# Five of eight gate pairs of two branches as seven block products for eight

## The chip, the cores and the metric
## The reference
Two layers over 512 prompt rows and 64 sample rows (together T = 576 columns), 1024 wide. A layer computes a projection `h @ w_in` into three branches (mLSTM, gMLP, sliding-window attention) and three sets of 1024 gates; each branch is projected to 1024, gated and summed; then an output projection and a SwiGLU feed-forward network (FFN) follow. What the change touches are the gates:

```python
gates = jax.nn.sigmoid(gl).reshape(B, S, N_BRANCH, D_MODEL)
merged = (gates[:, :, 0] * (y_ml @ p['w_br_mlstm'])
          + gates[:, :, 1] * (y_sg @ p['w_br_gmlp'])
          + gates[:, :, 2] * (y_sw @ p['w_br_swa']))
x = x + g1 * rms_norm(merged @ p['w_out'], p['g_post_mix'])
```

`gl` is the part of `h @ w_in` from column 3848 on: three times 1024 columns.

## The kernel before
Features lie on the 128 partitions, the 576 rows of both inputs along them in two halves of 288. A float32 product is made of three products of rounded parts: high by high, high by low, low by high. So each weight chunk (1024 x 128, 512 KB) is loaded by SyncE's queue into one of two raw buffers, split by GpSimd into a high part (L882) and a low part (L885), and used by TensorE in 8 x 3 x 2 = 48 matmuls of 128x288 (`main`, through `feature_group`, L971). A chunk's raw buffer is loaded again when its split is done. A gate chunk `g1_3` is the fourth 128 features of the second branch's gates. Gates come in pairs. Behind a pair stands its branch chunk: 512 x 256 weights, split in the same way, used in two groups of 24 matmuls (`br1_2` and `br1_3`).

For each gate, ScalarE takes a tanh of PSUM into the buffer `tmp` (L1899; a sigmoid is made from it), and VectorE merges: (tanh + 1) x branch in PSUM (L2886), and that added to `mid` (L2313, the line of a helper which records every tensor_tensor). In the second branch (sliding window, in the code `sw`, number 1) a spatial product of the third branch (`spatial`, L1625, `z0` to `z3`) follows each pair of gates; ScalarE writes its bias to PSUM first (`z_bias`, L2077), VectorE multiplies the result, ScalarE and VectorE round it into `y_hi` and `y_lo`.

PSUM has four units of two banks each, used in a fixed ring (`MIX` gives the order, `UNIT` the unit). Every engine has its own program, in order; semaphores join them. The order of each is written out in the code.

In the FFN stage most of the first projection runs in another form: for a pair of 128-feature outputs and two halves of the columns, the 2x2 block product of weights (blocks a11, a12, a21, a22; 512 KB each pair half) by activations is made of seven block products p1 to p7 (Winograd's form of Strassen's) in place of eight. Its operands are sums and differences of weight blocks (s1 to s4, made for each pair by VectorE) and of activation quarters (t1 to t4, made once a layer), each split into a high part (ScalarE, L2138 and L2151 for weights, L2125 for activations) and a low part (GpSimd for a11, a12, a22, L898; VectorE for the sums). A product is 4 x 3 matmuls of 288 columns (`product`, L1063), a pair 84; partial results are copied from PSUM by ScalarE (L2165) and added by VectorE.

## Time and profile before
| what | value |
|---|---|
| median of three runs | 2061.83 us (2061.35 to 2062.76) |
| profiled execution | 2064.86 us |
| its span, first to last instruction | 2063.1 us |
| TensorE busy | 2030.5 us (98%), 16241 matmuls |
| VectorE, ScalarE, GpSimd busy | 987.8, 624.9, 1064.4 us |
| mean granted TensorE clock | 0.998 |
| plain matmuls (L971) on the chain that ended last | 43% of the span |

The profile lists groups of instructions by line, with their busy time and the idle time before them; the chain that ended last, which is what the time is made of; and, on query, instructions in order of time. Matmuls overlap, so one of 128x288 is listed with 0.29 us though one follows the other every 0.133 us. Times are from the start of the span.

### The profile page before, as it was taken

The numbers are of one execution on the slowest core, as the hardware profiler recorded it, in microseconds if no ns is written. First come the engines' busy times: TensorE is split into PE (matmuls) and PEld (weight loads), VectorE is DVE, ScalarE is ACT, GpSimd is POOL, SyncE is SP. The second block draws the span as 40 slices with busy tenths as digits, with TensorE's granted clock in tenths as the row PEclk, the third lists the DMA queues.
The fourth block names the chain that finished last, engine by engine and source line by source line (L and its number), as shares of the span: only waits on it lengthen the run. The fifth ranks groups of instructions, "written<-read, shape, count | busy, mean of one in ns | idle before, by whom it ended". The sixth has DMA issues, their size and how long they took to land.

```text
span 2063.1 us, 38507 instructions
## 1 busy us (share of the span) xinstructions
PE 2030.5 (98%) x16241; PEld 1959.7 (95%) x16241; DVE 987.8 (48%) x1645; ACT 624.9 (30%) x1358; POOL 1064.4 (52%) x562
## 2 busy tenths in 40 slices
PE   8999999999999999999999999999999999999998
PEld 6998898999999999999999989889999999999997
DVE  5223466422257535647563235663223573647473
ACT  4111224110134333425532121340102343525253
POOL 0443454567763745363734534546687546354543
PEclk9999999999999999999999999999999999999999
DMA  9746232233351333233535342222233413232332
GB/s 358 259 137 52 63 82 59 68 83 86 90 182 42 126 121 92 83 92 93 174 121 174 62 63 76 62 59 75 82 103 89 148 43 91 82 89 85 94 93 77
DMA packets 299771, 211.93 MB, mean 103 GB/s; under 512 B 13728, under 2 KB 293840, under 8 KB 296400
## 3 DMA queue, kind: packets, MB, share of 16 engines
q1 hardware_dynamic: 292848, 205.94, 34.8%
q10 hardware_dynamic: 6752, 3.53, 0.7%
q8 instruction: 129, 2.11, 0.4%
q14 instruction: 42, 0.34, 0.1%
HBM read 204.65 MB, written 4.07 MB: 101 GB/s over the span
## 4 chain that ended last, share of the span: by engine, by line
PE 93%; DMA 2%; DVE 2%; POOL 1%; ACT 1%; issue 1%; SPq 0%; DVEq 0%; POOLq 0%; ACTq 0%
PE ps L971 43%; PE ps L1063 19%; PE ps L999 13%; PE ps L1083 3%; DMA raw<-in_w_in 2%; PE ps L1089 2%; PE ps L1216 2%; PE ps L1131 1%; PE ps L1595 1%; PE ps L1558 1%; PE ps L1573 1%; PE ps L1431 1%; PE ps L1259 1%; PE ps L1110 1%; PE ps L1446 1%
## 5 line engine op out<-in xcount | busy, mean ns | idle before, releaser
L971 PE MATMUL ps<-h_hi,hi_lo 128*128 128x288 f32 x3008 | 541.8, 298 | 1.7 <-POOL hi_lo L885 1.5
L882 POOL TENSOR_TENSOR hi_lo<-raw,consts 128x1024 fp32r<-128x1024 f32 (+1 forms) x124 | 236.8, 1910 | 473.6 <-PE ps L971 354.6
L971 PEld LDWEIGHTS ps<-h_hi,hi_lo 128*128 128x128 f32 x3008 | 446.9, 189 | 9.1 <-issue 5.1
L971 PE MATMUL ps<-h_lo,hi_lo 128*128 128x288 f32 x1504 | 322.2, 296 | 0.0
L885 POOL TENSOR_TENSOR hi_lo<-raw,hi_lo 128x1024 fp32r<-128x1024 f32 (+1 forms) x124 | 300.1, 2420 | 9.7
L898 POOL TENSOR_TENSOR a_lo<-raw,a_hi 128x512 fp32r<-128x512 f32 x108 | 159.2, 1474 | 271.5 <-ACT a_hi L2138 271.4
L971 PEld LDWEIGHTS ps<-h_lo,hi_lo 128*128 128x128 f32 x1504 | 242.6, 189 | 0.0
L999 PE MATMUL ps<-yf_hi,fo_h 128*128 128x288 f32 x704 | 152.5, 298 | 3.0 <-DVE yf_lo L2313 3.0
L1899 ACT ACTIVATE tmp<-ps 128x576 f32<-128x576 f32 x60 | 39.1, 652 | 382.3 <-PE ps L971 382.3
L882 POOL TENSOR_TENSOR hx<-raw,consts 128x1024 fp32r<-128x1024 f32 x34 | 68.4, 2010 | 160.3 <-PE ps L1089 65.1
L999 PE MATMUL ps<-yf_hi,fo_l 128*128 128x288 f32 x704 | 151.0, 296 | 0.0
L999 PE MATMUL ps<-yf_lo,fo_h 128*128 128x288 f32 x704 | 150.7, 296 | 0.0
L999 PEld LDWEIGHTS ps<-yf_hi,fo_h 128*128 128x128 f32 x704 | 112.9, 189 | 4.0 <-DVE yf_lo L2313 4.0
L913 POOL TENSOR_TENSOR fo_l<-raw,fo_h 128x768 fp32r<-128x768 f32 (+1 forms) x64 | 112.3, 1754 | 5.0
L999 PEld LDWEIGHTS ps<-yf_hi,fo_l 128*128 128x128 f32 x704 | 113.3, 189 | 0.3
L910 POOL TENSOR_TENSOR fo_h<-raw,consts 128x768 fp32r<-128x768 f32 (+1 forms) x64 | 90.9, 1420 | 43.6 <-PE ps L1063 17.8
L999 PEld LDWEIGHTS ps<-yf_lo,fo_h 128*128 128x128 f32 x704 | 113.2, 188 | 0.0
L2138 ACT ACTIVATE a_hi<-raw 128x512 fp32r<-128x512 f32 x108 | 67.9, 629 | 126.8 <-DMA raw<-in_w_ffn_in 85.2
L971 PE MATMUL ps<-y_hi,hi_lo 128*128 128x288 f32 x576 | 104.5, 298 | 0.0
L971 PE MATMUL ps<-h_hi,hx 128*128 128x288 f32 x400 | 86.8, 299 | 2.5 <-DVE ps L2476 1.4
L971 PEld LDWEIGHTS ps<-y_hi,hi_lo 128*128 128x128 f32 x576 | 85.3, 188 | 2.1 <-issue 1.6
L1063 PE MATMUL ps<-h_hi,s_lo 128*128 128x288 f32 x288 | 85.0, 295 | 0.9 <-DVE sq L2313 0.9
(398 smaller groups left out, 4554.5 us busy)
## 6 DMA issues: line engine op xcount, KB each, us to landing
raw<-in_w_in SPq DMA_DIRECT2D x108, 512.0 KB
ada<-in_w_ada SPq DMA_DIRECT2D x23, 2048.0 KB, 8.9
raw<-in_w_ffn_in SPq DMA_DIRECT2D x144, 256.0 KB, 3.1
raw<-in_w_ffn_out SPq DMA_DIRECT2D x32, 384.0 KB
raw<-in_w_ffn_out SPq DMA_DIRECT2D x32, 320.0 KB
raw<-in_w_out SPq DMA_DIRECT2D x16, 512.0 KB
raw<-in_w_ffn_in SPq DMA_DIRECT2D x16, 512.0 KB
raw<-in_w_br_mlstm SPq DMA_DIRECT2D x8, 512.0 KB
```

Source lines behind the costliest of these rows:

```text
L882: pool.tensor_tensor(hi, RAW[s][:, 0:size], ONES[:, 0:1].to_broadcast([128, size]), ALU.mult).then_inc(chunk_hi, 1)
L885: pool.tensor_tensor(lo, RAW[s][:, 0:size], hi.bitcast(f32), ALU.subtract).then_inc(chunk_split, 1)
L898: pool.tensor_tensor(lo[:, :], RAWB[o], hi[:, :].bitcast(f32), ALU.subtract).then_inc(s_alo, 1)
L910: pool.tensor_tensor(hi, RAW[s][:, 0:size], ONES[:, 0:1].to_broadcast([128, size]), ALU.mult).then_inc(chunk_hi, 1)
L913: pool.tensor_tensor(lo, RAW[s][:, 0:size], hi.bitcast(f32), ALU.subtract).then_inc(chunk_split, 1)
L971: m = pe.matmul(o[:, h, :], a[:, k, c0:c0 + 128], mv(k, h), start=(k == 0 and begins), stop=(k == nk - 1 and a is wl))
L999: m = pe.matmul(o[:, h, :], a[:, k * 128:(k + 1) * 128], mv(k, h), skip_group_check=c == LASTB, start=(k == 0 and begins and c < LASTB), s ...
L1063: m = pe.matmul(o, a[:, k * 128:(k + 1) * 128], mv(k), skip_group_check=True, start=(k == 0 and mv is bh and a is wh and p in ("p1", "p5", ...
L1083: pe.matmul(halves(l, nm)[:, h, :], a[:, k, :], HM[0](k, h), start=(x == 0 and a is wh), stop=False)
L1089: m = pe.matmul(halves(l, nm)[:, h, :], wh[:, k, :], HM[1](k, h), start=False, stop=(x == 7))
L1216: m = pe.matmul(unit(l, nm)[32 * x:32 * x + 32, 0:128], CS[:, k, :], wv[:, k, x * 128:(x + 1) * 128], start=(k == 0), stop=(k == 7))
L2138: act.activation(OPND[o][0][:, :], RAWB[o], ACT.Copy).then_inc(s_ahi, 1)
```

## The change
Three plain gate pairs stay in the second branch (`PLAIN1 = 3`); its fourth pair and all four of the third branch, five a layer (`GPAIRS`, numbered p = 0 to 4), are made as seven block products each. The gate pair's two raw buffers hold the four 256 KB blocks. The activation operands t1 to t4 are computed before the first of them. The four spatial products are made in the first two pairs, two behind each (`Z_AFTER`). Operands lie where the layer's earlier tensors were. Two PSUM units serve a pair (`ga`, whose second bank also holds the weight sums, and `gb`). TensorE's order, and the fixed order of ScalarE and VectorE, in the core of the diff:

```diff
+PLAIN1 = 3
+GPAIRS = [(1, n) for n in range(2 * PLAIN1, 8, 2)] + [(2, n) for n in range(0, 8, 2)]
+NGP = len(GPAIRS)
+Z_AFTER = {0: (0, 1), 2: (2, 3)}
...
+                def gate_block(o, p, g, n, pos):
+
+                    t, k0 = int(o[1] == "2"), 4 * (o[2] == "2")
+                    if (BRANCHES[2][1], n) == (g, 6):
+                        gate_blocks_read(o, l * NGP + p - 1)
+                    else:
+                        if p:
+                            gate_blocks_read(o, l * NGP + p - 1)
+                        sp.wait_ge(chunk_split, split_count(l, pos - 1 if (pos - 1) % 2 == t else pos - 2))
+                    sp.dma_start(RAWB[o].rearrange("p (k c) -> p k c", k=4),
+                                 w_in[:, k0:k0 + 4, ds(C_GL + g * D + (n + t) * 128, 128)]).then_inc(g_raw[o], 16)
...
+                for p, (b, n) in enumerate(GPAIRS):
+                    for o in ("a11", "a12", "a22"):
+                        gate_block_lo(o, p)
+                    if (b, n) != (2, 4):
+                        for pos in range(PAIR_AT[b, n] - ((b, n) == (2, 6)), PAIR_AT[b, n] + 1):
+                            split(pos)
...
+                def gate_begins(p, x):
+
+                    n = l * NGP + p
+                    if x == "p1":
+                        pe.wait_ge(unit_of(l, f"ga{p}"), empty(l, f"ga{p}"))
+                        pe.wait_ge(g_alo, 3 * n + 1)
+                    elif x == "p5":
+                        pe.wait_ge(unit_of(l, f"gb{p}"), empty(l, f"gb{p}"))
+                        pe.wait_ge(g_lo, 4 * n + 1)
+                        if p == 0:
+                            pe.wait_ge(gt_lo, nth(gt_lo, l, 0))
+                    elif x == "p6":
+                        pe.wait_ge(g_lo, 4 * n + 2)
+                        pe.wait_ge(g_kept, 3 * n + 1)
...
+                def gate_pair(p):
+
+                    gate_begins(p, "p1")
+                    for i, x in enumerate(PRODUCTS):
...
+                                if k == 3 and a is wl and i < 6:
+                                    gate_begins(p, PRODUCTS[i + 1])
...
+                def gate_keep(i, p):
+
+                    n = l * NGP + p
+                    first, second = GTILES[p]
+                    act.wait_ge(g_prod, gate_product(n, ("p1", "p5", "p6")[i]))
+                    if i == 0 and GPAIRS[p] != (2, 6):
+                        b, m = GPAIRS[p][0], GPAIRS[p][1] - 2
+                        if m < 0:
+                            b, m = b - 1, 6
+                        for e in range(2):
+                            act.wait_ge(unit_of(l, f"br{b}_{m + e}"), read(l, f"br{b}_{m + e}"))
+                    dst = (first[:, 0:HALF], second[:, HALF:T], first[:, HALF:T])[i]
+                    act.activation(dst, gate_rest(l, p)[:, 1, :] if i == 1 else gate_chain(l, p), ACT.Copy).then_inc(g_kept, 1)
...
+                def gate_weights(i, p):
+
+                    n, bank = l * NGP + p, gate_sum(l, p)
+                    if i == 1:
+                        dve.wait_ge(g_raw["a21"], 16 * (n + 1))
+                        dve.wait_ge(g_raw["a22"], 16 * (n + 1))
+                        dve.wait_ge(unit_of(l, f"ga{p}"), empty(l, f"ga{p}"))
+                        x = bank, RAWB["a21"], RAWB["a22"], ALU.add
+                    elif i == 2:
+                        dve.wait_ge(g_raw["a11"], 16 * (n + 1))
+                        dve.wait_ge(g_lo, 4 * n + 1)
+                        x = bank, bank, RAWB["a11"], ALU.subtract
...
+                    gate_c22(p)
+                    gate_first(p)
+                    if (b, n) == (2, 6):
+                        break
+                    gate_weights(1, p + 1)
+                    gate_weights_low(1, p + 1)
+                    gate_weights(2, p + 1)
+                    gate_weights_low(2, p + 1)
+                    merge(b, n)
+                    gate_weights(3, p + 1)
+                    gate_weights(4, p + 1)
+                    gate_weights_low(3, p + 1)
+                    merge(b, n + 1)
+                    gate_weights_low(4, p + 1)
```

How the instructions stand: VectorE from the third plain pair of the second branch on, in layer 0. The two rows that write `ps` and `mid` are a merge. Before:

```order
377 L2313 TENSOR_TENSOR wq<-mo_su,ps 128x576 [waits unit_free1,group_done]
378 L2313 TENSOR_TENSOR y_lo<-wq,y_hi 128x576 [waits yh_ready,unit_free3]
379 L2886 SCALAR_TENSOR_TENSOR ps<-tmp,ps 128x2x288 [waits group_done,unit_free1]
380 L2313 TENSOR_TENSOR mid<-ps,mid 128x576 [waits dve_step]
381 L2886 SCALAR_TENSOR_TENSOR ps<-tmp,ps 128x2x288 [waits chunk_used,unit_free2]
382 L2313 TENSOR_TENSOR mid<-ps,mid 128x576 [waits dve_step]
```

The last merge here is that of `br1_7`. In the changed kernel, around the merges of `br1_4` and `br1_5` (385 to 388), where t is an activation operand and g_s a weight sum's high or low part:

```order
384 L2538 TENSOR_TENSOR t2_lo<-t2_sum,t2_hi 128x1152 [waits gt_hi,gt_sum]
385 L3118 SCALAR_TENSOR_TENSOR ps<-tmp,ps 128x2x288 [waits group_done,unit_free2]
386 L2538 TENSOR_TENSOR mid<-ps,mid 128x576 [waits dve_step]
387 L3118 SCALAR_TENSOR_TENSOR ps<-tmp,ps 128x2x288 [waits chunk_used,unit_free3]
388 L2538 TENSOR_TENSOR mid<-ps,mid 128x576 [waits dve_step]
389 L2538 TENSOR_TENSOR t4_lo<-t4_sum,t4_hi 128x1152 [waits gt_hi,gt_sum]
390 L2538 TENSOR_TENSOR ps<-raw1 128x512 [waits unit_free2,g_raw_a22,g_raw_a21]
391 L2538 TENSOR_TENSOR g_s1_lo<-ps,g_s1_hi 128x512 [waits g_hi]
392 L2538 TENSOR_TENSOR h_lo<-t3_sum,h_hi 128x4x288 [waits gt_hi,gt_sum]
393 L2538 TENSOR_TENSOR ps<-ps,raw0 128x512 [waits g_lo,g_raw_a11]
394 L2538 TENSOR_TENSOR g_s2_lo<-ps,g_s2_hi 128x512 [waits g_hi]
395 L2538 TENSOR_TENSOR g_s3_sum<-raw0,raw1 128x512
```

The weight sums of the first product pair stand behind the last plain merge, and each sum into the PSUM bank behind the low part of the one before.

ScalarE, before, from the last spatial product's rounding to the third branch's gates: one tanh a gate and nothing between.

```order
227 L1899 ACTIVATE tmp<-ps 128x576 [waits chunk_used,unit_free0]
228 L1950 ACTIVATE y_hi<-wq 128x576 [waits unit_free3]
229 L1899 ACTIVATE tmp<-ps 128x576 [waits merged2,chunk_used,unit_free1,unit_free0]
230 L1899 ACTIVATE tmp<-ps 128x576 [waits chunk_used,merged2] x5
231 L1899 ACTIVATE sq<-ps 128x576 [waits chunk_used] x2
```

In the changed kernel, from the last tanh of one product pair (242) to the copies of the next pair's products (250, 251):

```order
242 L2265 ACTIVATE tmp<-ps 128x288 [waits g_prod]
243 L2228 ACTIVATE g_a11_hi<-raw0 128x512 [waits g_prod,g_raw_a11]
244 L2228 ACTIVATE g_a12_hi<-raw0 128x512 [waits g_prod,g_raw_a12]
245 L2236 ACTIVATE g_s1_hi<-ps 128x512 [waits g_prod,g_sum]
246 L2236 ACTIVATE g_s2_hi<-ps 128x512 [waits g_prod,g_sum]
247 L2236 ACTIVATE a11_hi<-g_s3_sum 128x512 [waits g_prod,g_sum]
248 L2228 ACTIVATE g_a22_hi<-raw1 128x512 [waits g_prod,g_raw_a22]
249 L2236 ACTIVATE g_s4_hi<-ps 128x512 [waits g_prod,g_sum]
250 L2251 ACTIVATE tmp<-ps 128x288 [waits unit_free1,unit_free0,g_prod]
251 L2251 ACTIVATE tmp<-ps 128x288 [waits g_prod] x2
```

Seven high parts of weights stand ahead of the copy of the first product, and that copy also waits for both merges of the pair before (`unit_free0`, `unit_free1`).

## Rows read from the trace of the kernel before

**Rows 1.** The page: span, busy time of the engines, chain that ended last.
```profile
span 2063.1 us, 38507 instructions
PE 2030.5 (98%) x16241; PEld 1959.7 (95%) x16241; DVE 987.8 (48%) x1645; ACT 624.9 (30%) x1358; POOL 1064.4 (52%) x562
PE 93%; DMA 2%; DVE 2%; POOL 1%; ACT 1%; issue 1%; SPq 0%; DVEq 0%; POOLq 0%; ACTq 0%
```

**Rows 2.** Stretch, its us; PE, PEld, DVE, ACT, POOL busy; clock; DMA; GB/s.
```profile
401.00:568.00 167.00, 167.00 (x1253) 166.25 (x1252) 39.38 (x50) 20.86 (x50) 116.41 (x54) 1.00 0.31 87
752.00:807.80 55.80, 55.80 (x423) 55.80 (x422) 38.10 (x52) 28.82 (x59) 24.68 (x18) 1.00 0.38 119
1411.00:1578.00 167.00, 167.00 (x1253) 166.25 (x1251) 39.82 (x50) 20.86 (x50) 116.36 (x54) 1.00 0.31 86
```

**Rows 3.** The chain in order of time: start us, us, what.
```profile
421.18 1.48 PE ps L1625 x12
485.27 83.40 PE ps L971 x624
...
752.03 55.77 PE ps L1063 x420
```

**Rows 4.** Instructions in order of time around a spatial product: start us, us.
```profile
415.42 1.11 ACT L2077 ACTIVATE ps<-b_spatial 128x128 f32<-128x128 f32 x6
421.01 1.64 PE L1625 MATMUL ps<-w_spatial_t,v_tok 128*128 128x128 f32 x12
421.27 0.65 ACT L1899 ACTIVATE tmp<-ps 128x576 f32<-128x576 f32 x1 [4.74 <-PE ps L971]
```

**Rows 5.** The same, activation operands of the FFN stage.
```profile
664.03 3.40 POOL L885 TENSOR_TENSOR lx<-raw,hx 128x1024 fp32r<-128x1024 f32 x1
665.75 2.89 DVE L2313 TENSOR_TENSOR t_sum<-mid,t_sum 128x1152 f32<-128x1152 f32 x1
689.21 1.34 DVE L2313 TENSOR_TENSOR h_lo_sum<-mid 128x1152 f32<-128x1152 f32 x1
```

**Rows 6.** The same, behind the first spatial product.
```profile
423.30 2.39 POOL L885 TENSOR_TENSOR hi_lo<-raw,hi_lo 128x1024 fp32r<-128x1024 f32 x1
424.26 2.04 DVE L2313 TENSOR_TENSOR y_lo<-wq,y_hi 128x576 fp32r<-128x576 f32 x1 [0.82 <-ACT y_hi L1950]
```

**Rows 7.** The same, the split for the sixth gate of branch two.
```profile
471.14 1.90 POOL L882 TENSOR_TENSOR hi_lo<-raw,consts 128x1024 fp32r<-128x1024 f32 x1 [3.71 <-PE ps L971]
473.12 2.39 POOL L885 TENSOR_TENSOR hi_lo<-raw,hi_lo 128x1024 fp32r<-128x1024 f32 x1
```

**Rows 8.** The same, first of a merge's two steps.
```profile
491.98 0.76 DVE L2886 SCALAR_TENSOR_TENSOR ps<-tmp,ps 128x576 f32<-128x576 f32 x1 [1.59 <-PE ps L971]
```

**Rows 9.** The same, one pair of the FFN stage.
```profile
764.79 0.41 ACT L2165 ACTIVATE tmp<-ps 128x288 f32<-128x288 f32 x1 [0.60 <-PE ps L1063]
765.10 0.59 ACT L2151 ACTIVATE s_hi<-ps 128x512 fp32r<-128x512 f32 x1
769.63 0.63 ACT L2138 ACTIVATE a_hi<-raw 128x512 fp32r<-128x512 f32 x1 [1.23 <-PE ps L1063]
...
769.20 0.70 DVE L2313 TENSOR_TENSOR ps<-raw 128x512 f32<-128x512 f32 x1 [0.89 <-DMA raw<-in_w_ffn_in]
777.62 0.68 DVE L2313 TENSOR_TENSOR s_lo<-ps,s_hi 128x512 fp32r<-128x512 f32 x1
```

**Rows 10.** Loads of 256 KB blocks: a late one on the chain, and all of them.
```profile
845.87 4.14 DMA raw<-in_w_ffn_in
...
DMA to landing us min/median/max: 2.6/3.1/5.2
```

**Rows 11.** TensorE's waits by releaser: us in total, times, longest.
```profile
PE ps L935 <- DMA consts<-in_consts: 3.2, 1, 3.2
...
PE ps L1259 <- issue: 1.8, 1, 1.8
```

More of the change, by code:

```diff
@@ L228 @@
 P_QK, P_WVIF, P_WK, P_V, P_MO, P_WQ, P_SU, P_SV, P_BR = 0, 6, 9, 10, 14, 18, 22, 26, 30
-P_WO = P_BR + 36
+PAIR_AT, _p = {}, P_BR
+for _b_ in range(3):
+    for _n in range(0, 8, 2):
+        PAIR_AT[_b_, _n] = _p
+        _p += 1 if (_b_, _n) in GPAIRS else 3
+P_B2, P_WO = PAIR_AT[2, 0], _p
 P_FFN = P_WO + 8
@@ L1652, in _ @@
+                for n in range(0, 8, 2):
+                    pos = PAIR_AT[1, n]
+                    if (1, n) in GPAIRS:
+                        gate_pair(GPAIRS.index((1, n)))
+                        branch(1, n, pos)
+                        continue
                     for e in range(2):
                         main(f"g1_{n + e}", pos + e)
-                    spatial(n // 2)
+                    for g in Z_AFTER.get(n, ()):
+                        spatial(g)
                     if n == 0:
@@ L2078, in z_bias, with gt_high, gate_block_high @@
                     m.then_inc(zb_ready, 1)
-                for n in range(0, 8, 2):
-                    g = n // 2
+                def gt_high(i, dst, src):
+                    act.wait_ge(gt_sum, nth(gt_sum, l, (2, 5, 7, 4)[i]))
+                    act.activation(dst, src, ACT.Copy).then_inc(gt_hi, 1)
+                def gate_block_high(o, p):
+                    n = l * NGP + p
+                    act.wait_ge(g_raw[o], 16 * (n + 1))
+                    if p:
+                        act.wait_ge(g_prod, gate_product(n - 1, {"a11": "p1", "a12": "p2", "a22": "p4"}[o]))
+                    act.activation(GOPND[o][0][:, :], RAWB[o], ACT.Copy).then_inc(g_ahi, 1)
@@ new lines, in gate_tanh @@
+                def gate_tanh(i, p):
+                    n = l * NGP + p
+                    first, second = GTILES[p]
+                    if i == 0:
+                        act.wait_ge(g_c22, n + 1)
+                        act.activation(second[:, HALF:T], second[:, HALF:T], ACT.Tanh, scale=0.5).then_inc(g_tanh, 1)
+                    elif i == 1:
+                        act.wait_ge(unit_of(l, f"gb{p}"), read(l, f"gb{p}"))
+                        act.activation(first, first, ACT.Tanh, scale=0.5).then_inc(g_tanh, 1)
+                    else:
+                        act.wait_ge(g_prod, gate_product(n, "p4"))
+                        act.activation(second[:, 0:HALF], gate_chain(l, p), ACT.Tanh, scale=0.5)                            .then_inc(unit_of(l, f"ga{p}"), 1)
@@ L2090, in _ @@
-                for n in range(8):
-                    if n < 6:
-                        act.wait_ge(merged2, before(merged2, l, n))
-                    tile(f"g2_{n}", TS[:, n % 2, :] if n < 6 else SQ[:, n - 6, :], ACT.Tanh, 0.5)
+                    if zs:
+                        z_bias(zs[1])
+                    for g in zs:
+                        act.wait_ge(unit_of(l, f"z{g}"), read(l, f"z{g}"))
+                        y_hi(4 + g, WQ[:, 2 + g % 2, :])
+                    if 3 in zs:
+                        gt_high(0, T1H[:, :, :], T1SUM[:, :, :])
@@ L2906, in _, with whole @@
                     x += 1
-                for n in range(0, 8, 2):
-                    g = n // 2
-                    nm = f"z{g}"
-                    dve.wait_ge(done_by(nm), done(l, nm))
-                    dve.wait_ge(unit_of(l, f"su{g}"), read(l, f"su{g}"))
-                    tt(split2(WQ[:, 2 + g % 2, :]), split2(SU[:, g, :]), halves(l, nm), ALU.mult).then_inc(unit_of(l, nm), 1)
-                    dve.wait_ge(unit_of(l, nm), read(l, nm))
-                    y_lo(4 + g, WQ[:, 2 + g % 2, :])
-                    for e in range(2):
-                        merge(1, n + e)
+                def whole(i, dst, k, h):
+                    if i == 6:
+                        dve.wait_ge(tables_loaded, 16 if l == 0 else 48)
+                    tt(dst, h_part(HH, k, h).bitcast(f32), h_part(HL, k, h).bitcast(f32), ALU.add).then_inc(gt_sum, 1)
@@ L2927, in merged_lo @@
                         dve.memset(SCRATCH[:, 0:1], 0.0).then_inc(unit_of(l, f"br2_{k}"), 1)
-                for n in range(4):
-                    merge(2, n)
-                dve.wait_ge(done_by("g2_7"), done(l, "g2_7"))
+                dve.wait_ge(g_prod, 7 * NGP * (l + 1))
                 merged_lo(0)
```

296 lines of the change are left out of this document (245 added, 51 removed).

## The prediction
> **What bounds the kernel now.** I read four views, in this order. First the page: TensorE is busy for 2030.5 of 2063.1 us, and 93% of the chain that ended last is TensorE's [rows 1]. So TensorE is the bound, and what it is given to do is time, as long as the others keep up. Second, busy time by stretch, over the part that the change rewrites, gates and branches two and three: from 401 to 568 us, and in the second layer from 1411 to 1578, TensorE is busy for 167.00 of 167.00 us, at a granted clock of 1.00 (2.4 GHz) [rows 2]. There is no gap to win back; any wait that the change brings is new time. GpSimd is busy for 116 of the 167 us, VectorE for 39, ScalarE for 21 [rows 2]: on average there is room, so the question is one of order and latency. Third, the FFN stage, which already runs pairs in the seven-product form: 420 products take 55.77 us there without a gap, with VectorE at 38.1 and ScalarE at 28.8 of 55.8 us [rows 2, 3]. That is the evidence for the change: the form can run dense. Fourth, the instructions in order of time of VectorE, ScalarE and GpSimd, for what one step lasts and how long a chain of them is [rows 4 to 9].
>
> **What is removed.** A plain pair is 96 matmuls of 288 columns. A matmul costs 83.40/624 = 133.65 ns in the plain form and 55.77/420 = 132.8 ns in the product form [rows 3]. A pair goes from 96 x 0.13365 = 12.83 to 84 x 0.1328 = 11.15 us: 1.68 us less. Five pairs a layer, two layers: **-16.8 us**. The branch groups (24 matmuls, 3.2 us each, two behind each pair) stay.
>
> **What is moved: the spatial products.** Each second of them needs its bias in PSUM. ScalarE now writes it behind the second gate's tanh. Before, it stood behind the first gate's, 6.4 us ahead. TensorE begins the first spatial product at 421.0; the tanh starts at 421.27, frees ScalarE after 0.55 us, and the bias takes 1.11 us [rows 4]: ready at 422.93, seen by TensorE at about 423.05. The first spatial product covers 1.48 us, to 422.5 [rows 3]. 0.55 us, twice a layer: **+1.1 us a layer**.
>
> **What is added: the sums of the activations.** Eight sums or differences and four low parts of 128x1152 a layer on VectorE; such a one takes 1.34 us in the FFN stage [rows 5]. Both inputs lie in SBUF, and there VectorE and GpSimd exclude each other. The low part that begins at 424.26 should take 0.7 us and ends at 426.30, 0.6 us after GpSimd's split ends (423.30 + 2.39 = 425.69) [rows 6]; a sum from 665.75 ends at 668.64, when GpSimd's, delayed itself by a low part of VectorE's, has ended at 667.43 [rows 5]. So the twelve take turns with the splits. They stand in line from the last spatial product on; a split (1.90 + 2.39 us, after which 1.8 us remain before its gate is due [rows 7]) gets up to two such turns of 1.3 us put into it. The splits for the sixth gate and for the third branch pair come 0.6 and 0.4 us late, and the first low part of the weights 0.4 us: **+1.4 us a layer**.
>
> **The first pair.** The first fence of the order shows the cause. VectorE is in line behind the merge of the last plain branch group, which can't begin before TensorE has ended that group; call that moment 0. Merge, two steps of 0.76, to 1.8 [rows 8]; low part of the fourth activation operand 1.3, to 3.1; first weight sum 0.6 to 3.7; its high part on ScalarE 0.6 and its low part 0.7, to 5.1 [rows 9]. TensorE is there with all but one matmul of its first product at 1.5, or 1.9 with the 0.4 above: it stops for **3.3 us**. Then the sums use one PSUM bank in turn, each waiting for the low part before it: activation low part 1.3, second sum 0.7, high 0.65, low 0.7, third and fourth sum 1.3; then ScalarE does the high parts of the third, of a22 and of the fourth, 1.6 us, and only then copies the first product out (0.41): 11.1. The third product needs that copy, and TensorE has been waiting for it since 6.9: **4.2 us**. Sum 7.5 a layer. What is late next (fourth sum's low part, a22's) is in time.
>
> **The pairs after a branch.** Three a layer. Let E be the end of a pair's products. TensorE then runs two branch groups, the first product and all but one matmul of the second: 6.4 + 1.6 + 1.5 = E + 9.45. There it needs the copy of the first product, which the second fence shows behind seven steps of ScalarE, and which waits for the previous merge too, as it overwrites the tile. The chain: last tanh E + 0.7, which frees the bank; sum 0.7, high 0.65, low 0.7, sum 0.7, high 0.65, low 0.75; merge 1.5; third and fourth sum 1.3; low 0.6; second merge 1.6; copy 0.5: E + 10.6, and 0.1 to TensorE. **1.3 us** late, with every load in time. In the FFN stage the two sums lie in two banks, the sums are not held by a merge, and VectorE still waits 0.89 us for a block before its first sum [rows 9]; that is why it runs dense there and why I don't carry that over.
> Loads: a block of the next pair can't overwrite a buffer before the branch chunk in it is split. That chunk is itself loaded only after a22's low part (256 KB land in 2.6 to 5.2 us, median 3.1 [rows 10]; I take 3.2 for 512 KB), and its split takes 4.3 us. In the second pair this puts the split 0.4 us behind the branch group's need, and a21 and a22, issued behind it, at E + 3.8, for a sum that could start at E + 0.7: +2.2 us after what is taken up by the 0.4. The third pair has them in time, the fourth at E + 2.4: +1.6. In the fourth, ScalarE's steps for the fifth pair stand between the copies and wait for blocks: +1.3. So 0.4 + 3.5, 1.3, 2.9 + 1.3 = **9.4 us a layer**. The fifth pair's sums are made during the fourth: no wait. GpSimd's two last splits end 2.8 us before and 4.8 us before they are needed: no wait at the output projection.
>
> **Sum.** 1.1 + 1.4 + 7.5 + 9.4 = 19.4 us a layer, 38.8 in all, less 16.8: **+22.0 us**. The profiled execution took 2064.86 us, 3.0 over the median of the runs, so it would be 2086.9 and the median 2061.83 + 22.0 = **2083.8 us**. Bounds: with all loads in time and no turns lost the cost is 1.1 + 7.5 + 3 x 1.3 = 12.5 a layer, +8 us in all, 2070. With blocks landing 0.8 us later (the 4.14 us of [rows 10]), each pair that waits for them waits longer, in the fourth the whole delay twice: 24.4 a layer, +32 us, 2094. I take the middle, because the median landing is nearer to 3.1.
>
> **The clock.** The trace shows 1.00 in every stretch around the stage [rows 2], and TensorE never idles for more than 3.2 us in it, after its first instructions for 1.8 [rows 11]; the stalls of 3.3 and 4.2 us, with 1.6 us of work between, are longer.
> The Trainium skill ("TensorE: Matmul & The Clock Gate", the section on how the clock gate bites in real kernels) says that an engine left idle long enough between bursts falls back to half its clock and has to earn it again; by it the sum would be larger, as in the first rival. No row here shows such a fall.
>
> **Rivals.**
> 1. *The stalls drop the clock.* A matmul at 1.2 GHz costs 0.133 us more. The bound is both stalled pairs of a layer at that level all through: 2 x 84 x 0.133 = 22.3 us a layer, less what hides in the next stall. A quarter of it, 5.6 a layer: 2084 + 11 = 2095. For it: stalls that are longer than any of before. Against: no row at the lower level. Chance 0.10.
> 2. *Only the start of the stage waits* (a wait that the later pairs hide). The copy and the merge would have to be 1.3 us quicker than I add them up, and the loads too. Then 10.0 a layer, 20 - 16.8 = +3.2 us, 2065: within what can't be told or just over. For it: GpSimd and ScalarE are idle most of the time [rows 2]. Against: the chain is made of steps each of which has a row. Chance 0.11, of which 0.06 within 0.2%.
> 3. *The helpers keep up, as in the FFN stage.* VectorE's sums and the merge overlap with the first product, no stall is over a few tenths; only the bias stays. -16.8 + 2.2 = -14.6 us, 2047. It decides against me if VectorE gets to the first weight sum before the last plain merge, 3.6 us earlier than by its order; but the order is fixed. For it: 420 products without a gap [rows 3]. Chance 0.07.
> The change does have 12 matmuls fewer a pair in the order of TensorE's instructions; that it wouldn't save them is no case.
>
> **How the numbers follow.** Forecast, 2070 to 2094: 0.72; the rivals 0.10, 0.11 and 0.07. About 0.2%, 4 us, is what a measurement of this kernel can tell from no change. Faster 0.07, same 0.06, slower 0.87. The range reaches from 2067 to 2094, which leaves out the two lower cases and half of the first rival.
>
> **What would show it.** In the changed kernel TensorE's waits in the stage should name VectorE's weight low parts (two of about 3.3 us, in the first pair) and ScalarE's copy of a product into the gate tile (eight, 1.3 to 4.2 us, the largest sum), and the busy time from the first gate of branch two to the output projection should be 167 - 8.4 us within a stretch 11 us longer than before. The two second biases should cost 0.5 us each. The prediction is wrong if the stretch is shorter than 167 us, if the copy is not what TensorE waits for in the pairs after a branch, or if the clock falls.

## The result, and the profile after

| what | before | changed |
|---|---|---|
| median of four runs | 2061.59 us (2060.82 to 2062.76) | 2094.86 us (2091.68 to 2096.62) |
| ratio | | 1.0159, 95% interval 1.0142 to 1.0177 |
| profiled execution, its span | 2064.86, 2063.1 us | 2096.62, 2094.8 us |
| mean granted TensorE clock | 0.998 | 0.990 |

The change makes the kernel 33.3 us slower. The forecast was 2083.8 us, with a range up to 2094.0: the direction is right, the size is 11.1 us short, and the time lies 0.9 us above the range.

In the changed kernel L1779 are the matmuls of the product pairs, L1060 the plain ones, L1714 the spatial ones, L2251 the copies of a product into the gate tile, L2214 the bias, L2538 all two-operand steps of VectorE. The page [rows 1]:
```profile
span 2094.8 us, 38683 instructions
PE 2031.4 (97%) x16121; PEld 1956.9 (93%) x16121; DVE 1088.8 (52%) x1769; ACT 685.9 (33%) x1476; POOL 1025.6 (49%) x552
```
TensorE has 120 matmuls fewer and is busy for longer. The busy time by stretch answers that [rows 2] (columns as there). First both layers' stage whole, then pieces of it:
```profile
401.00:585.00 184.00, 168.55 (x1201) 165.85 (x1200) 92.20 (x112) 51.47 (x109) 92.75 (x48) 0.95 0.27 76
1428.00:1611.00 183.00, 166.02 (x1203) 163.46 (x1202) 92.55 (x114) 52.18 (x111) 95.51 (x49) 0.97 0.28 77
...
478.00:480.00 2.00, 1.23 (x5) 1.26 (x6) 2.00 (x3) 0.00 (x0) 0.00 (x0) 0.70 0.00 0
480.00:482.00 2.00, 1.98 (x9) 1.63 (x7) 1.34 (x3) 0.60 (x1) 0.00 (x0) 0.50 0.00 0
...
508.00:512.00 4.00, 4.00 (x18) 4.00 (x18) 0.00 (x0) 0.82 (x2) 3.37 (x2) 0.50 0.40 111
520.00:524.00 4.00, 4.00 (x32) 4.00 (x31) 2.84 (x5) 0.92 (x2) 2.02 (x2) 1.00 0.00 0
```
The clock was 1.00 throughout [rows 2]; now it is 0.95 and 0.97. From 508 us TensorE starts 18 matmuls in 4 us at 0.50 (1.2 GHz), from 520 it starts 32 at 1.00. Both stretches count as fully busy, so busy time hides this; the counts and the clock show it. TensorE's waits [rows 11] (releaser: us in total, times, longest):
```profile
PE ps L1779 <- ACT tmp L2251: 10.3, 4, 3.9
PE ps L1779 <- DVE g_s_lo L2538: 7.6, 2, 3.8
PE ps L1779 <- DVE a_lo L2538: 6.6, 2, 4.0
PE ps L1779 <- issue: 6.2, 2, 3.1
...
PE ps L1714 <- ACT ps L2214: 1.3, 4, 0.3
```
The releaser named is the one whose event came last. In the pair at 507 the copy ends at 507.52 and VectorE's last low part at 507.59, so the row goes to the low part. The program tells which one it is: ahead of the third product TensorE waits for the second low part (`g_lo`), done at 502.08, and for the copy of the first product (`g_kept`), and not for the last low part. So this is a wait for the copy, and so are the two that the rows give to `a_lo`, where the copy ends 0.1 us ahead of the matmul. The eight waits for the copy are 25.9 us together. What the copy waits for, in the pairs behind a branch, is the second merge (`mid`); ScalarE's seven steps had ended 1.30 us before:
```profile
507.11 0.41 ACT L2251 ACTIVATE tmp<-ps 128x288 f32<-128x288 f32 x1 [1.30 <-DVE mid L2538]
```
The first stall, named "issue", is the wait for the first weight sum's low part. VectorE around it, in order of time, and TensorE:
```profile
474.69 0.76 DVE L2538 TENSOR_TENSOR mid<-ps,mid 128x576 f32<-128x576 f32 x1
475.36 1.35 DVE L2538 TENSOR_TENSOR t_lo<-t_sum,t_hi 128x1152 fp32r<-128x1152 f32 x1
476.63 0.69 DVE L2538 TENSOR_TENSOR ps<-raw 128x512 f32<-128x512 f32 x1
477.98 0.69 DVE L2538 TENSOR_TENSOR g_s_lo<-ps,g_s_hi 128x512 fp32r<-128x512 f32 x1 [0.66 <-ACT g_s_hi L2236]
```
```profile
478.77 0.56 PE L1779 MATMUL ps<-h_hi,g_a_lo 128*128 128x288 f32 x1 [3.12 <-issue]
479.14 0.44 PE L1779 MATMUL ps<-t_hi,g_s_hi 128*128 128x288 f32 x1
479.38 0.44 PE L1779 MATMUL ps<-t_lo,g_s_hi 128*128 128x288 f32 x1
...
484.56 0.37 PE L1779 MATMUL ps<-t_hi,g_s_lo 128*128 128x288 f32 x1 [2.59 <-DVE a_lo L2538]
```
Merge, activation low part, first sum, its low part: the chain of the prediction. Behind the stall a matmul follows the other every 0.24 us, where it was every 0.133 [rows 3].

The stalls, as the distance between two starts less 0.133 us. Layer one: 0.46 and 0.46 (spatial), 0.35 (a11's low part), 3.28 and 2.90 (first pair), 3.97, 1.31, 4.10 (second to fourth): 16.8 us. Layer two: 0.46, 0.46, 0.37, 3.27, 4.12, 3.96, 1.44, 4.10: 18.2. The matmuls 0.2 to 0.3 us apart took 6.7 and 4.6 us over 0.133 each. 35.0 + 11.4 - 16.8 = +29.6 us, less the 1.0 us of such matmuls that before has too: +28.6. Seven matmuls 0.3 to 0.4 us apart, five of them the second start behind a stall, add 1.6. The stage, from its first spatial matmul to one and the same matmul of the output projection, measures +30.5 (next section); the executions differ by 31.8.

### The profile page after: what moved, and what is told of

It is laid out like the page before. It is cut to its first block, busy times and chain, and to the rows that moved or that the text cites. A ratio compares the mean times of both kernels' runs of the same rounds, so it can differ in the third digit from the quotient of the medians.

```text
span 2094.8 us, 38683 instructions
## 1 busy us (share of the span) xinstructions
PE 2031.4 (97%) x16121; PEld 1956.9 (93%) x16121; DVE 1088.8 (52%) x1769; ACT 685.9 (33%) x1476; POOL 1025.6 (49%) x552
## 4 chain that ended last, share of the span: by engine, by line
PE 84%; DVE 5%; issue 3%; DMA 3%; POOL 2%; ACT 2%; SPq 0%; DVEq 0%; ACTq 0%; POOLq 0%
PE ps L1060 32%; PE ps L1152 19%; PE ps L1088 13%; PE ps L1779 3%; PE ps L1172 3%; DMA raw<-in_w_in 2%; PE ps L1178 1%; PE ps L1305 1%; PE ps L1220 1%; DVE t_sum L2538 1%; PE ps L1520 1%; PE ps L1684 1%; PE ps L1647 1%; PE ps L1535 1%; PE ps L1662 1%
## 5 line engine op out<-in xcount | busy, mean ns | idle before, releaser
L1060 PE MATMUL ps<-h_hi,hi_lo 128*128 128x288 f32 x2560 | 463.0, 299 | 0.3 <-POOL hi_lo L959 0.2
L956 POOL TENSOR_TENSOR hi_lo<-raw,consts 128x1024 fp32r<-128x1024 f32 (+1 forms) x112 | 218.6, 1951 | 447.4 <-PE ps L1060 319.2
L1060 PEld LDWEIGHTS ps<-h_hi,hi_lo 128*128 128x128 f32 x2560 | 380.5, 189 | 8.0 <-issue 5.3
L959 POOL TENSOR_TENSOR hi_lo<-raw,hi_lo 128x1024 fp32r<-128x1024 f32 (+1 forms) x112 | 274.7, 2452 | 8.8
L1060 PE MATMUL ps<-h_lo,hi_lo 128*128 128x288 f32 x1280 | 274.4, 296 | 0.0
L1060 PEld LDWEIGHTS ps<-h_lo,hi_lo 128*128 128x128 f32 x1280 | 206.4, 189 | 0.0
L956 POOL TENSOR_TENSOR hx<-raw,consts 128x1024 fp32r<-128x1024 f32 x26 | 53.1, 2044 | 149.5 <-PE ps L1178 65.5
L1060 PE MATMUL ps<-y_hi,hi_lo 128*128 128x288 f32 x640 | 115.4, 297 | 0.0
L2036 ACT ACTIVATE tmp<-ps 128x576 f32<-128x576 f32 x44 | 28.6, 651 | 219.0 <-PE ps L1060 219.0
L1060 PEld LDWEIGHTS ps<-y_hi,hi_lo 128*128 128x128 f32 x640 | 94.8, 188 | 1.9 <-issue 1.6
L970 POOL TENSOR_TENSOR g_a_lo<-raw,g_a_hi 128x512 fp32r<-128x512 f32 x30 | 38.4, 1292 | 108.8 <-ACT g_a_hi L2228 108.8
```

Source lines behind the costliest of these rows:

```text
L956: pool.tensor_tensor(hi, RAW[s][:, 0:size], ONES[:, 0:1].to_broadcast([128, size]), ALU.mult).then_inc(chunk_hi, 1)
L959: pool.tensor_tensor(lo, RAW[s][:, 0:size], hi.bitcast(f32), ALU.subtract).then_inc(chunk_split, 1)
L970: pool.tensor_tensor(lo[:, :], RAWB[o], hi[:, :].bitcast(f32), ALU.subtract).then_inc(g_alo, 1)
L1060: m = pe.matmul(o[:, h, :], a[:, k, c0:c0 + 128], mv(k, h), start=(k == 0 and begins), stop=(k == nk - 1 and a is wl))
```

## The experiments

One measure serves all: the length of the stage. It begins with the first spatial matmul (421.01 and 1430.51 us before, 421.04 and 1446.43 changed) and ends where this piece of the chain starts, of before and of the changed kernel:
```profile
587.77 29.03 PE ps L971 x216
1597.26 29.03 PE ps L971 x216
```
```profile
603.66 29.03 PE ps L1060 x216
1627.86 29.03 PE ps L1060 x216
```
| kernel | stage, layers one and two, us | over before | medians: over before of the same series |
|---|---|---|---|
| before | 166.76, 166.75 | | |
| changed | 182.62, 181.43 | +30.5 | +33.3 |
| e1_filler | 180.12, 179.74 | +26.4 | 2087.65 - 2062.99 = +24.7 |
| e2_bias | 182.07, 182.35 | +30.9 | 2093.59 - 2063.35 = +30.2 |
| e3_pairs | 171.96, 174.05 | +12.5 | 2076.88 - 2062.99 = +13.9 |
| e4_start | 175.46, 177.43 | +19.4 | 2086.34 - 2062.99 = +23.4 |
| e5_all | 165.46, 167.72 | -0.3 | 2064.39 - 2062.99 = +1.4 |
| e8_apart | 161.95, 162.39 | -9.2 | 2055.69 - 2063.35 = -7.7 |

**1. Matmuls of no use in the stalls** (e1_filler).
```diff
+ def fill(o, count, w, mv):
+     for i in range(count):
+         pe.matmul(o, w[:, 384:512], mv(3), skip_group_check=True, start=True, stop=True)
...
  if k == 3 and a is wl and i < 6:
+     if x == "p1" and p == 0:
+         pe.wait_ge(unit_of(l, f"gb{p}"), empty(l, f"gb{p}"))
+         fill(gate_rest(l, p)[:, 1, :], 22, wl, mv)
+     if x == "p5" and p < 4:
+         fill(gate_rest(l, p)[:, 0, :], [20, 24, 8, 24][p], wl, mv)
      gate_begins(p, PRODUCTS[i + 1])
```

> The changed kernel with matmuls of no use put into its stalls: 22 ahead of the last matmul of the first product of a layer's first product pair, and 20, 24, 8 and 24 ahead of the last matmul of the second product of pairs one to four. They write a PSUM half that the next product starts anew, at 0.133 us each: 2.9, 2.7, 3.2, 1.1 and 3.2 us in places where TensorE stood for 3.3, 2.9 to 4.1, 4.0, 1.3 and 4.1. Nothing that the kernel computes is changed. Theory A (the stalls are also what dropped TensorE's clock to 0.50, and the 11.4 us that the matmuls of the half-clock stretches took over their 0.133 us are the term missing in the sum): what is left of each stall is under 1.5 us, the granted clock stays 1.00 through the gates of both layers, and the time falls from 2094.9 by some 11 us less what of the stalls was made of them, to 2081 to 2086. Theory B (the stalls alone are the cost, the low clock beside them is of another cause or costs nothing): 2094 to 2096, as TensorE is released by the same helpers at the same moments, with the half-clock stretches still there.

Measured: 2087.65 us, ratio 1.0119 (1.0104 to 1.0134), against 1.0159. The clock where it was 0.50 (508 us), and where the longest stall begins:
```profile
478.00:480.00 2.00, 1.80 (x14) 1.83 (x15) 1.97 (x3) 0.00 (x0) 0.00 (x0) 1.00 0.00 0
508.00:512.00 4.00, 4.00 (x33) 4.00 (x32) 0.46 (x1) 0.42 (x2) 3.33 (x2) 1.00 0.01 3
```
No stretch of the stage is below 1.00, no stall over 1.61 us. So it is the stalls that drop the clock: 26 us of matmuls that compute nothing were added, and the kernel got faster. But it gave back 7.2 us between the two medians (8.6 by the last column of the table) and 4.2 by the stage, and not 11: theory A is right in kind and too large. Of the time of the slow matmuls some 6 us had run beside the helpers' chains and so shortened the next stall (stalls and fillers together are 41.3 us here, the stalls were 35.0): the second stall of the first pair was 2.90 us with slow matmuls ahead, and is 20 x 0.133 + 1.47 = 4.13 without. The run also measures the stalls with the clock taken out: what is left, 7.70 and 7.53 us, plus 98 x 0.133 = 13.0 a layer, is 20.7 and 20.6, where the prediction had 19.4.

**2. Both biases first** (e2_bias). In ScalarE's order `z_bias(zs[1])` goes from behind the second gate's tanh to ahead of it.

> The changed kernel with one step moved: both biases of a pair of spatial products are written ahead of the second gate's tanh, as the one was before the change. Theory A (the wait of TensorE is ScalarE's second bias alone): the four stalls of 0.46 us are gone, and nothing returns: 2094.9 - 1.8 = 2093. Rival (the stage behind is held by helpers that do not start earlier, GpSimd's splits): 0.6 of the 1.8 comes back at the first product pair, 2093.5 to 2094.5. The time hardly tells these apart, the trace's stalls do.

Measured: 2093.59 us, ratio 1.0149 (1.0135 to 1.0163). The four stalls of 0.46 us are gone from the trace, and the one for a11's low part ahead of the first pair grows from 0.35 to 1.09: the rival's return, 0.74 of 0.92 a layer. It is a wait for GpSimd's low part (0.92 of it idle):
```profile
PE ps L1779 <- POOL g_a_lo L970: 1.8, 2, 0.9
```
The medians don't tell the two apart. The clock falls behind all eight stalls of 3.1 us and more, also behind the one of a pair of layer two (3.12 us) whose like in the changed kernel (3.27) left it at 1.00.

**3. Another order between pairs** (e3_pairs). Steps of pair p + 1, VectorE's and ScalarE's; W and L are weight sum and low part, M a merge, A and S high parts of blocks and sums, K1 the copy of the first product:
```diff
- VectorE: W1 L1 W2 L2 M0 W3 W4 L3 M1 L4     ScalarE: A11 A12 S1 S2 S3 A22 S4 K1
+ VectorE: W1 L1 W2 W3 L2 M0 M1 W4 L3 L4     ScalarE: S1 A11 A12 S2 A22 S3 K1 S4
```

> The changed kernel with other orders of VectorE and ScalarE from one pair to the next, and the same instructions. ScalarE copies the first product out sixth of its eight steps and not last (first sum, a11, a12, second sum, a22, third sum, COPY, fourth sum); VectorE makes the third weight sum ahead of the second low part and its two merges ahead of the fourth weight sum. Beside the fourth pair the copies of its products stand ahead of the second and third high parts of the fifth. The first pair of a layer is as it was. Theory A (a stall behind a branch is the chain of helper steps ahead of the copy, and it also drops the clock): the stalls of pairs two to four fall from 4.0, 1.3 and 4.1 us to about 1.5 to 1.8, 0.1 and 0.2 to 0.6, 6.5 us a layer less, 13 in all; with them go the half-clock stretches at pairs two and four, some 7 of the 11.4 us. 2075. The low clock stays at the first pair. Theory B (stalls without a price of the clock): 2082. Theory C (the loads of the blocks, not the order, hold those stalls, as the prediction put it for 3.5 of the second pair and 2.9 of the fourth): only the parts of 1.3 us go, 2 to 4 us a layer, 2086 to 2091.

Measured: 2076.88 us, ratio 1.0066 (1.0051 to 1.0081): 18 us gone by an order alone. The stalls of pairs two to four are 1.19, none, 1.08 + 0.40 in layer one and 1.49, 0.38 + 0.69, 1.40 + 0.33 in layer two, where they were 3.97, 1.31 to 1.44, 4.10. The clock is at 1.00 behind them and still falls at the first pair:
```profile
486.00:488.00 2.00, 2.00 (x10) 2.00 (x10) 0.00 (x0) 0.41 (x1) 0.11 (x1) 0.52 1.09 351
504.00:508.00 4.00, 3.92 (x29) 3.95 (x30) 1.30 (x3) 1.31 (x3) 0.23 (x1) 1.00 0.69 208
508.00:512.00 4.00, 4.00 (x33) 4.00 (x32) 1.21 (x2) 0.78 (x2) 3.92 (x2) 1.00 0.23 59
```
Theory C, that the loads hold these stalls, falls: the blocks come no sooner (VectorE waits 3.26 us for them ahead of its first sum, of the changed kernel 3.30), and 2.5 to 2.8 of the 4.0 us go all the same. The same sum in both, changed kernel first:
```profile
496.95 1.62 DVE L2538 TENSOR_TENSOR ps<-raw 128x512 f32<-128x512 f32 x1 [3.30 <-DMA raw<-in_w_in]
```
```profile
496.11 0.70 DVE L2529 TENSOR_TENSOR ps<-raw 128x512 f32<-128x512 f32 x1 [3.26 <-DMA raw<-in_w_in]
```
It also ran without the 0.9 us that it lost beside a step of GpSimd (from 495.47 for 2.53 us; in e3_pairs that step starts at 498.04), which is part of the 2.8. ScalarE is idle for 2.88 us ahead of this pair's copy and waits for the second merge, so for this stall it is VectorE's order that counts, the merges ahead of the fourth sum; the two orders were not tried one by one. The fourth pair's steps were reordered as well, as expected above.

**4. Another order at the start** (e4_start). G are sums of activations, GL their low parts, M12 to M15 the merges of the plain pairs; ScalarE's high parts are reordered to match:
```diff
- ... M12 G3 G4 M13 G5 G6 G7 GL0 GL1 M14 M15 GL2 W1 L1 GL3 W2 L2 W3 W4 L3 L4
+ ... M12 G3 M13 G4 G5 G6 W1 G7 M14 GL0 M15 L1 W2 GL1 W3 L2 GL3 GL2 L3 W4 L4
```

> The changed kernel with another order at the start of the pairs alone. VectorE makes the first, second and third weight sums of the first pair, and their low parts, ahead of or between the last two low parts of the activations, and the first of them ahead of the merge of the last plain branch group; ScalarE makes the first high parts of the weights ahead of the last two of the activations. The later pairs are as they were. Theory A: the stalls of the first pair (3.3 and 2.9 to 4.1 us) become three of 1.0 to 1.9 us (first sum's low part, second sum's, copy of the first product), 3 us a layer shorter together; the second pair's falls from 4.0 by up to 2.5, since its blocks are loaded earlier. 6 us a layer, 12 in all, and the half-clock stretches of the first pair go: 2078 to 2082. Theory B (no price of the clock): 2083. Theory C (the start is held by the merge and GpSimd's split and not by VectorE's order): the same stalls one step later, 2092 to 2096.

Measured: 2086.34 us, ratio 1.0111 (1.0096 to 1.0126). The first pair's stalls are 1.08, 1.55 and 1.72 (layer two 1.61, 1.57, 1.73), as theory A had them, and the clock holds there. But the second pair's stall, expected at about 1.5, is 2.73 and 3.98: an earlier start of the first pair does little for the chain behind it. That is most of the 4 to 8 us by which A was too low.

**5. Both orders and both biases** (e5_all).

> Both new orders together, at the start of the pairs and between them, and both biases of the spatial products written ahead of the second gate's tanh, where the first stood before the change. Same instructions, same products. By the rows: 0.2 us before a branch group, then 1.4, 1.6 and 1.9 us in the first pair, none in the four later ones: 5 us a layer where the five pairs save 8.4. Theory A (stalls are all of the loss, and those of 2.9 us and more are what the clock falls on): no half-clock stretch, 2 x (5.0 - 8.4) = -6.7 us against the kernel before: 2055, range 2051 to 2060. Theory B (something beside the stalls makes the product form dearer here than in the FFN stage, as longer matmuls or a lower clock without a stall): not faster than before, 2060 to 2070. Theory C (the clock falls on several stalls of 1.5 us in a row too): 2055 and 2 to 4 us for the first pair of each layer, 2057 to 2063.

Measured: 2064.39 us (ten runs, 2059.99 to 2067.62), ratio 1.0007 (0.9997 to 1.0016): the loss is gone, a gain isn't there. The number alone would fit theory B; the sum of the stage below doesn't leave room for it. The trace has no half-clock stretch in the stage, against C. But it is the trace of the fastest of the ten executions (2059.99 us, mean clock 0.999); the others took 2062.50 to 2067.62 at 0.996 to 0.997, the level of before in this series, and where they lose it no trace shows. The first pair is as summed (1.08, 1.56, 1.73), but the later ones still stop TensorE for 2.05 and 4.1 us a layer, all for the copy of the first or third product:
```profile
PE ps L1787 <- ACT tmp L2259: 5.0, 7, 1.5
PE ps L1787 <- issue: 5.0, 4, 1.6
...
PE ps L1787 <- DVE g_s_lo L2531: 2.8, 2, 1.4
```
The product form costs nothing beside its stalls: 166.76 + 166.75 - 16.8 + 14.9 (the stalls) = 331.6 us, and the stage measures 333.2.

**6 to 9. The price of a stall by itself.** On the kernel before, ScalarE holds TensorE at chosen gates by copying a free tile onto itself:
```diff
+ if (b, n) in HELD:                      # ScalarE, ahead of the gate's tanh
+     act.wait_ge(done_by(f"g{b}_{n}"), done(l, f"g{b}_{n}"))
+     for _ in range(3):                  # 6, 4, 12 in the others
+         act.activation(TS[:, n % 2, :], TS[:, n % 2, :], ACT.Copy).then_inc(held, 1)
+         own[0] += 1
+         act.wait_ge(held, own[0])
...
+ if (b, n) in HELD:                      # TensorE, behind that gate's matmuls
+     pe.wait_ge(held, l * HELD_STEPS + 3 * (HELD.index((b, n)) + 1))
```

> The price of the clock by itself, on the kernel before: TensorE is made to wait at four points a layer (behind the first gate group of the first and third gate pair of branch two and of the first and third of branch three), each time until ScalarE has copied a free 128x576 tile onto itself three times, ahead of that gate's tanh. A 128x576 step of ScalarE takes 0.65 us there, so each wait is 3 x 0.66 + 0.2 = 2.2 us, eight of them 17.6 us. Theory A (TensorE's clock falls only behind a stall of nearly 3 us or more; the stalls of 1.3 and 1.4 us of the changed kernel left it at 1.00): no half-clock stretch, 2079 to 2081. Theory B (any stall of this size has it fall): each costs 1.4 to 1.7 us more, 2090 to 2094.

> The same total of waiting in half as many stalls: on the kernel before, two waits a layer (first gate pair of branch two, third of branch three), each for six copies of the tile: 6 x 0.66 + 0.2 = 4.2 us, four of them 16.8 us. TensorE has work without a gap on both sides of them. Theory A (a stall of 4 us drops the clock, and the matmuls behind it then run at half speed with nothing to hide them): four half-clock stretches of 1.4 to 1.7 us each, 6 to 7 us on top of the stalls: 2084 to 2087, above the short waits though it waits less. Theory B (the low clock of the changed kernel needs more than one such stall, or costs nothing): 2078 to 2080, some 1 us under the short waits.

> As the kernel with four short waits a layer, each of four copies of the tile where those had three: the short waits came out at 2.43 us (three copies), the long ones at 4.84 (six), so 3.2 us each, eight of them 25.8 us. With three copies one stall in four was followed by a half-clock stretch (1.9 us), with six every one (2.2 us). Theory A (the longer the stall, the surer the fall, and the price of one is 1.9 to 2.2 us at any length): at 3.2 us at least two of four fall, as most stalls of 2.9 to 4.1 us did in the changed kernel: 4 to 8 falls, 8 to 17 us on top: 2063.4 + 25.8 + 8 to 17 = 2097 to 2106. Theory B (what decides is where the stall stands, and not its length): again only the fourth of a layer: 2063.4 + 25.8 + 3.8 = 2093.

> One wait a layer, of twelve copies, behind the first gate group of the third pair of branch two, on the kernel before: about 12 x 0.8 = 9.6 us at the step of the two other kernels (2.41 us more for three copies), 19.3 us in all. Theory A (a fall costs 1.9 to 2.2 us, however long the stall): 2063.4 + 19.3 + 4.4 = 2087. Theory B (the price grows with the stall, since more of what follows runs at half speed: 2.2 us at 4.8, so 4.4 at 9.7): 2091 to 2093.

| kernel | stalls, us each | falls of the clock | price of a fall, us | sum in both layers | measured |
|---|---|---|---|---|---|
| e6_idle_short | 8 x 2.43 | 2 of 8 | 1.6, 1.6 | +21.3 | 2084.49 - 2063.35 = +21.1 |
| e9_idle_middle | 8 x 3.14 | 8 of 8 | 1.4 to 2.8, mean 2.1 | +41.8 | 2102.71 - 2061.63 = +41.1 |
| e7_idle_long | 4 x 4.57 | 4 of 4 | 2.2 to 2.8, mean 2.5 | +28.2 | 2090.63 - 2063.35 = +27.3 |
| e10_idle_once | 2 x 8.86 | 2 of 2 | 2.6, 1.3 | +21.6 | 2083.34 - 2061.63 = +21.7 |

(TensorE's instructions are those of before, so starts compare matmul by matmul: the price is how much later than in before it is 12 us behind a stall, less the stall; the sum is how much later it is at the output projection than ahead of the first stall.) Busy time by stretch behind a long stall, a short one that ends at 459.61, and one of e9_idle_middle:
```profile
416.00:418.00 2.00, 0.00 (x0) 0.00 (x0) 0.00 (x0) 1.93 (x3) 2.00 (x1) 0.58 0.00 0
418.00:420.00 2.00, 1.82 (x7) 1.82 (x8) 0.00 (x0) 1.77 (x8) 0.24 (x1) 0.50 0.30 70
420.00:422.00 2.00, 2.00 (x10) 2.00 (x10) 0.00 (x0) 0.00 (x0) 0.00 (x0) 0.50 0.68 201
422.00:424.00 2.00, 2.00 (x13) 2.00 (x13) 0.00 (x0) 0.00 (x0) 0.00 (x0) 0.71 0.00 0
```
```profile
460.00:462.00 2.00, 2.00 (x18) 2.00 (x17) 0.00 (x0) 1.24 (x7) 1.86 (x1) 1.00 0.00 0
462.00:464.00 2.00, 2.00 (x18) 2.00 (x17) 0.00 (x0) 0.00 (x0) 0.00 (x0) 1.00 0.49 130
```
```profile
464.00:466.00 2.00, 2.00 (x10) 2.00 (x9) 0.00 (x0) 0.00 (x0) 0.00 (x0) 0.50 0.61 143
```
Four long stalls cost 6 us more than eight short ones of about the same total (18.3 and 19.4 us). A fall costs 2.1 us in the mean, and its price doesn't grow with the stall: it spreads as much at one length (1.4 to 2.8 behind 3.14 us) as over all. In e10_idle_once the 0.50 lasted 5.5 us behind one stall (2.6 us) and 3.0 behind the other (1.3). So e9 and e10 go to theory A, e10 some 4 us under its number. The four runs of e9_idle_middle lie far apart, 2094.91 (mean clock 0.993) to 2109.77 us (0.984): the 8 of 8 holds for the profiled execution, and the fastest run suggests fewer falls. The expectations of the first two were low: the stalls came out longer (2.43 for 2.2, 4.57 for 4.2), two of the short ones did drop the clock, and the 1.4 to 1.7 us a fall, read from the changed kernel, is 2.5 in e7_idle_long, where nothing hides it.

**10. The weight sums out of one bank's line** (e8_apart). For pairs two to five:
```diff
+ def gate_outer_sum(l, p):
+     return SQ[:, 1, T - WH:T] if p else gate_sum(l, p)
...
-     x = bank, bank, RAWB["a11"], ALU.subtract          # second sum, behind the first's low part
+     x = bank, outer, RAWB["a11"], ALU.subtract         # behind the first sum alone
...
-     x = bank, RAWB["a12"], bank, ALU.subtract          # fourth
+     x = outer, RAWB["a12"], bank, ALU.subtract
- VectorE between pairs: W1 L1 W2 W3 L2 M0 M1 W4 L3 L4
+ VectorE between pairs: W1 W2 W3 L1 W4 M0 M1 L2 L3 L4
```

> The changed kernel with both biases first, and with the four weight sums of pairs two to five no longer in line for one PSUM bank: the first and fourth are written to a free part of a VectorE tile in SBUF, the second to the bank, the third where it was. So the second sum waits for neither the high nor the low part of the first. The orders of VectorE and ScalarE are new again (at the start the first low part of the weights is made ahead of the last two merges, between pairs the first three sums stand in a row). The run with both new orders left stalls of 4.4 us in the first pair and of 2.0 to 4.1 in the later ones. Theory A (what was left there is the chain of sums and loads ahead of the copy): 0.2 before a branch group, 0.7 and 2.3 in the first pair, up to 0.9 in the second, under 0.3 in the others: 4.1 to 4.7 us a layer, 2 x (4.4 - 8.4) = -8 us: 2054 by the rows, and since the run of both orders came out 5 us over the same sum, 2055 to 2060. Theory B (the loads alone hold what was left, since the blocks land later than I take them): no faster than the run with both orders, 2062 to 2066.

Measured: 2055.69 us, ratio 0.9960 (0.9947 to 0.9972): it beats both kernels, by 0.4% and, over the two ratios, 2%. VectorE between the first two pairs, and TensorE's waits in the pairs of both layers:
```profile
485.36 0.69 DVE L2538 TENSOR_TENSOR sq<-raw 128x512 f32<-128x512 f32 x1 [3.88 <-DMA raw<-in_w_in]
486.18 0.70 DVE L2538 TENSOR_TENSOR ps<-sq,raw 128x512 f32<-128x512 f32 x1
486.79 0.68 DVE L2538 TENSOR_TENSOR g_s_sum<-raw 128x512 f32<-128x512 f32 x1
487.39 0.69 DVE L2538 TENSOR_TENSOR g_s_lo<-sq,g_s_hi 128x512 fp32r<-128x512 f32 x1
```
```profile
PE ps L1791 <- DVE g_s_lo L2538: 5.9, 4, 2.1
```
The load is still waited for (3.88 us), and then the sums run back to back. The stalls are 2.23 and 0.98 us in layer one, 2.23 and 1.13 in layer two. The buffers and the orders changed together, so how much each brought of the gain over experiment 5, some 9 us, was not measured. The profiled execution is again the fastest (2050.69 us, clock 0.999; the others 2054.11 to 2057.00 at 0.995 to 0.997).

## Why the prediction came out short

- *The clock*: the step that failed, and by the prediction's own words ("or if the clock falls"). The paragraph wrote "No row here shows such a fall", left the clock out of the sum and gave it 0.10. Seven of the eight stalls of 2.9 us or more drop it (not the one of 3.27 us at 1504); this cost 4 us by the stage and 7 to 9 by the medians (experiment 1). The rival's own size, 11 us over the forecast, landed on the time to 0.1 us, but partly by chance: its price was a quarter of a bound, and the true sum is a smaller clock term and larger stalls. That all rows lay at 1.00 was weak evidence: the stretches of [rows 2] have no wait in them, the 3.2 us of [rows 11] stand at the kernel's first matmuls and the next longest is 1.8, and the forecast stalls lay above both. And the trace of before has a fall, outside the stage and in none of the rows, behind 23 matmuls of 4x4 and 4x1 (L1471 and L1473) and without any wait:
```profile
126.00:128.00 2.00, 2.00 (x25) 1.99 (x25) 0.23 (x3) 0.59 (x1) 1.89 (x1) 1.00 0.20 58
128.00:130.00 2.00, 2.00 (x12) 2.00 (x11) 0.37 (x6) 0.00 (x0) 1.98 (x1) 0.60 0.00 0
```
So "no row at the lower level" was true of the rows and not of the trace. The Trainium skill's rule ("TensorE: Matmul & The Clock Gate", on how the gate bites in real kernels), which the prediction quoted and set aside, is in kind what happened in the stage (granted 0.50 behind seven of the eight).
- *The first pair*: 3.3 measured 3.28; 4.2 measured 2.90 and 4.12, and 4.13 once the clock held. Right, with its chain.
- *Spatial products*: 2 x 0.55 measured 2 x 0.46. Right, mis-sized by 0.2 a layer.
- *Turns with GpSimd*: 1.4 a layer measured 0.35 beside the waits for the biases, and 1.09 once those are gone (experiment 2). Biases and turns were added, 1.1 + 1.4, where one hides the other: 1.27 together. The turns themselves show in rows: GpSimd's second split step at 457.24 took 3.39 us for 2.39, and the sum of 1.62 us above was at 0.7 in the prediction. Leaving the activation sums out was not tried, so the turns have no experiment.
- *The pairs after a branch*: 9.4 a layer measured 9.4 and 9.5 (3.97 + 1.31 + 4.10; 3.96 + 1.44 + 4.10) beside a low clock. With the clock at 1.00 (experiment 1, fillers counted) the second is 4.1 and 4.3 for 3.5, the third 1.3 and 1.4 for 1.3, the fourth 6.4 and 5.6 for 4.2, and the branch groups ahead 0.5 and 0.6 for 0.4: this term was 2.7 us a layer too small, and the agreement above is that of two errors. With every load in time (the third pair) the chain is right: the copy ends at 528.78, 10.6 us behind the end of the pair at 518.19, though the steps as listed add up to 10.35. For the second pair the prediction put the blocks at E + 3.8 and counted 2.2 of the 3.1 us behind E + 0.7; the 0.4 that it names doesn't make up the difference. The first sum came at E + 2.7 (E is 494.27), the fourth pair's at E + 2.9 for 2.4. What was missed is how much a step takes beside GpSimd (0.9 us in the second pair), and the third product's copy in the fourth pair. The split into causes was wrong as well: 5.1 us were put down to late loads as a fixed delay, and experiment 3 shows the same loads with 6 us a layer less. A late load costs what stands between it and TensorE, and that was the order.
- *What is removed*: 16.8 us. Right: in experiment 5 the stage is within 1.6 us of before, less 16.8, plus its stalls.
- *Rival 3* (helpers keep up) named the point that decides: the first weight sum ahead of the last plain merge. True as a cure of the first pair only (experiment 4); it took three edits more to get under before.

Of the 11.1 us, 8.5 lie in the stage (+30.5 for +22.0): 4.2 the clock, 5.3 the pairs after a branch, -2.5 biases and turns, and 1.5 that no experiment isolates, in part the second start behind a wait, which comes some 0.07 us late at full clock too. The rest is between the stage and the medians (+33.3), which differ by -1.7 to +4.0 us in the table above, and stays open: the stage is read from one execution each, and those of one kernel differ by some microseconds and in their mean clock.

## What to carry to other kernels

A stall on the engine that bounds has two prices: its length, and, behind stalls like those of 2.9 us and more here, about 2 us more for the clock; so eight stalls of 2.4 us cost less than four of 4.6. Where a dense form saves 1.7 us a pair, it pays only if the helpers' chain from "operand buffer free" to "product may start" is shorter than the work that TensorE has in hand: count that chain's steps before the matmuls. When a stall is long, move first what doesn't feed the late step behind it, and give sums that need not share a buffer their own.
